# A two-model forward pass on one core: the first layer's index stage with its low products, key scalings, score relus and bias table copy in another order

## What is computed

```
proj = h @ w_in
q = rms_norm(proj[..., :o1].reshape(b, s, A_HEADS, A_HEAD_DIM), q_gain)
k = rms_norm(proj[..., o1:o2], k_gain)
v = proj[..., o2:o3]
qi = proj[..., o3:o4].reshape(b, s, IDX_HEADS, IDX_DIM)
ki = proj[..., o4:o5]
wi = proj[..., o5:]
...
dots = jnp.einsum('bqhd,bsd->bqhs', qib, ki).astype(jnp.float32) * (IDX_DIM ** -0.5)
score = jnp.einsum('bqh,bqhs->bqs', wib.astype(jnp.float32) * (IDX_HEADS ** -0.5),
                   jax.nn.relu(dots))
score = jnp.where(admiss[None], score, NEG)
_, idx = lax.top_k(score, n_top)
...
bias = rel_bias[t5_bucket(idx - t[None, :, None])]
logits = logits + jnp.transpose(bias, (0, 3, 1, 2)).astype(jnp.float32)
```

## Time and profile before

| what | value |
|---|---|
| median of 3 runs | 1145.93 us (1145.24 to 1149.59) |
| profiled execution, its own time | 1146.56 us |
| its span in the profile | 1144.8 us |
| mean granted TensorE clock | 0.993 |
| TensorE matmul busy | 1115.6 us, 97% |
| TensorE weight load busy | 988.1 us, 86% |
| VectorE busy | 709.9 us, 62% |
| ScalarE busy | 583.5 us, 51% |
| GpSimd busy | 147.3 us, 13% |
| moved by DMA | 193.96 MB, mean 169 GB/s |

### The profile page before, as it was taken

One profiled execution on the slowest core, in us unless ns is written; L12 is line 12 of the kernel. 1 busy time (PEld: TensorE's weight loads), 2 busy tenths in 40 slices (PEclk: granted clock), 3 DMA queues, 4 the chain that ended last, 5 costly groups with the idle time before them and its releaser, 6 DMA issues.

```text
span 1144.8 us, 17804 instructions
## 1 busy us (share of the span) xinstructions
PE 1115.6 (97%) x7045; PEld 988.1 (86%) x7045; DVE 709.9 (62%) x995; ACT 583.5 (51%) x767; POOL 147.3 (13%) x106
## 2 busy tenths in 40 slices
PE   8999999999998999999999999999999999999997
PEld 7768888888887888888888999898899989999996
DVE  5863665656677646555556978476587655554554
ACT  5574644444677554444455546445546346443443
POOL 3534200000364240000030000000000022000001
PEclk9999999999998999999999999999999999999999
DMA  7927465555341236555555655437554444655552
GB/s 232 302 67 182 162 218 188 185 201 187 117 145 67 84 113 223 199 191 193 183 162 169 221 153 166 129 118 239 178 165 138 159 151 156 211 181 188 188 175 90
DMA packets 138782, 193.96 MB, mean 169 GB/s; under 512 B 7147, under 2 KB 112840, under 8 KB 138716
## 3 DMA queue, kind: packets, MB, share of 16 engines
q1 hardware_dynamic: 126796, 181.92, 48.9%
q10 hardware_dynamic: 11312, 11.05, 3.6%
q0 software_dynamic: 608, 0.08, 0.1%
HBM read 191.90 MB, written 6.37 MB: 173 GB/s over the span
## 4 chain that ended last, share of the span: by engine, by line
PE 81%; DVE 7%; ACT 6%; issue 2%; DMA 2%; POOL 1%; SPq 0%; ACTq 0%; DVEq 0%
PE psum L546 20%; PE psum L547 19%; PE psum L548 19%; PE psum L707 11%; PE psum L708 5%; ACT arena L1553 3%; PE psum L635 2%; ACT whi L1567 2%; DVE wlo L2123 2%; DMA raw<-in_a_w_in 2%; POOL wlo L1536 1%; PE psum L1265 1%; PE psum L1238 1%; PE psum L666 1%; DVE psum L2492 1%
## 5 line engine op out<-in xcount | busy, mean ns | idle before, releaser
L1567 ACT ACTIVATE whi<-raw 128x2048 fp32r<-128x2048 f32 (+2 forms) x174 | 325.8, 1874 | 259.7 <-PE psum L548 163.8
L2123 DVE TENSOR_TENSOR wlo<-raw,whi 128x2048 fp32r<-128x2048 f32 (+1 forms) x148 | 337.8, 2284 | 190.0 <-ACT whi L1567 189.0
L546 PE MATMUL psum<-xA,whi 128*128 128x256 f32 x840 | 240.5, 286 | 4.3 <-POOL wlo L1536 2.0
L547 PE MATMUL psum<-xA,whi 128*128 128x256 f32 x840 | 238.3, 284 | 0.0
L548 PE MATMUL psum<-xA,wlo 128*128 128x256 f32 x840 | 238.2, 284 | 0.0
L1536 POOL TENSOR_TENSOR wlo<-raw,whi 128x288 fp32r<-128x288 f32 (+3 forms) x57 | 117.2, 2082 | 805.2 <-ACT whi L1567 805.0
L707 PE MATMUL psum<-xA,whi 128*128 128x512 f32 x512 | 182.9, 400 | 0.1
L546 PEld LDWEIGHTS psum<-xA,whi 128*128 128x128 f32 x840 | 161.0, 192 | 7.9 <-DVE wlo L2123 3.8
L547 PEld LDWEIGHTS psum<-xA,whi 128*128 128x128 f32 x840 | 161.2, 192 | 0.7
L548 PEld LDWEIGHTS psum<-xA,wlo 128*128 128x128 f32 x840 | 161.1, 192 | 0.1
L546 PE MATMUL psum<-whi,xC 128*128 128x512 f32 (+1 forms) x384 | 149.7, 390 | 1.1 <-DVE xC L2432 1.1
(11 more groups left out here) (272 smaller groups left out, 1343.8 us busy)
## 6 DMA issues: line engine op xcount, KB each, us to landing
raw<-in_w_in SPq DMA_DIRECT2D x42, 1024.0 KB, 5.2
raw<-in_mlp_w_up SPq DMA_DIRECT2D x32, 1024.0 KB, 5.4
raw<-in_mlp_w_down SPq DMA_DIRECT2D x32, 1024.0 KB, 4.9
raw<-in_w_gate SPq DMA_DIRECT2D x11, 1024.0 KB, 5.3
raw<-in_w_up SPq DMA_DIRECT2D x11, 1024.0 KB, 5.3
raw<-in_w_down SPq DMA_DIRECT2D x11, 1024.0 KB, 4.9
raw<-in_a_w_in SPq DMA_DIRECT2D x6, 1024.0 KB, 7.1
raw<-in_a_w_o SPq DMA_DIRECT2D x4, 1024.0 KB, 4.9
```

The source lines that it names most:

```text
L546: nc.tensor.matmul(out, lh, rh, start=start, stop=False, skip_group_check=skip)
L547: nc.tensor.matmul(out, lh, rl, start=False, stop=False, skip_group_check=skip)
L1567: nc.scalar.activation(whi[c % N_SPLIT][:, 0:n], raw[c % N_RAW][:, 0:n], ACT.Copy).then_inc(hi_sem, 1)
L2123: V.tensor_tensor(wlo[c % N_SPLIT][:, 0:n], raw[c % N_RAW][:, 0:n], f(whi[c % N_SPLIT][:, 0:n]), ALU.subtract).then_inc(lo_sem["dve"], 1)
```

## The change

On TensorE, `qi0` is written out: all its high products (L866 of the new program, 32) come first and wait only for the high part of the weights; its 16 low products (L871) follow. The scores of heads 4 to 7 are computed behind the first query block of `q0a` and no longer before it, and the banks of `queries` are opened one by one. On ScalarE, the root of the key mean stands ahead of the splits of `qi1` and `q0a`; the relus of heads 0 and 1 stand ahead of the split of `q0b`; the skew copy is issued behind the relus of heads 2 and 3; the reading back into `toep` is issued behind the split of `q1b` and no longer before it. On VectorE, the low part of `qi1` comes behind the key scalings and the key mean.

```diff
@@ -856,7 +856,22 @@
-            feature_major("qi0", xA, 5)
+            c = index["qi0"]
+            hi, lo = slot(c, KT, 256)
+            pe.wait_ge(hi_sem, c + 1)
+            out = open_bank("qi0.0", 5)
+            for nt in range(2):
+                for k in range(KT):
+                    for part in range(2):
+                        nc.tensor.matmul(out[:, nt * 256:nt * 256 + 256], hi[:, k, nt * P:nt * P + P], xA[:, part, k, :],
+                                         start=nt == k == part == 0, stop=False, skip_group_check=True)
+            weights(c)
+            for nt in range(2):
+                for k in range(KT):
+                    ins = nc.tensor.matmul(out[:, nt * 256:nt * 256 + 256], lo[:, k, nt * P:nt * P + P], xA[:, 0, k, :],
+                                           start=False, stop=k == KT - 1, skip_group_check=True)
+            close_bank(ins, "qi0.0")
+            chunk_done[c] = full["qi0.0"]
@@ -885,17 +900,23 @@
             feature_major("qi1", xA, 1, between=first_dots)
-            wait_read("qi1.0")
-            dots((4, 5, 6, 7), (4, 5, 0, 2))
-
-            def queries(j, banks, before_last=None):
-
-                outs = [open_bank(f"q{j}.{blk}", b) for blk, b in enumerate(banks)]
+
+            def last_dots():
+                wait_read("qi1.0")
+                dots((4, 5, 6, 7), (4, 5, 0, 2))
+
+            def queries(j, banks, before_last=None, behind_first=None):
+
+                outs = []
                 for part in range(2):
                     c = index[f"q{j}{'ab'[part]}"]
                     hi, lo = slot(c, 4, 512)
                     weights(c)
                     for blk in range(NB):
+                        if not part:
+                            if blk and behind_first:
+                                behind_first()
+                            outs.append(open_bank(f"q{j}.{blk}", banks[blk]))
@@ -917,7 +938,7 @@
-            queries(0, (3, 6))
+            queries(0, (3, 6), None, last_dots)
@@ -1694,11 +1715,9 @@
             run(sd, ms, ACT.Sqrt, done["A.sd"])
-            split_to("q0a")
-            act.wait_ge(s_tab, 16)
-            shift_rows(tab_a, skew_a, 16)
             act.wait_ge(*done["A.k.ms"])
             run(hd[:, 0:2], hd[:, 0:2], ACT.Sqrt, done["A.k.sd"])
+            split_to("q0a")
@@ -1713,16 +1732,20 @@
             run(vecs[:, :], psum[:, bank["vecs"], 0:V_ROWS], ACT.Copy, read["vecs"])
+            index_relu(0)
+            index_relu(1)
             split_to("q0b")
-            for h in range(4):
-                index_relu(h)
+            index_relu(2)
+            index_relu(3)
+            act.wait_ge(s_tab, 16)
+            shift_rows(tab_a, skew_a, 16)
             evac_a("qi1.0", A["qiT"][:, 2:4, :])
             for h in range(4, IDX_HEADS):
                 index_relu(h)
             split_to("q1a")
+            split_to("q1b")
             act.wait_ge(s_skew, 16)
             act.dma_start(A["toep"], skew_a.ap().rearrange("h p s -> p h s")).then_inc(s_toep_a, 16)
-            split_to("q1b")
@@ -2251,7 +2274,6 @@
             run(V.reciprocal(rs, sd), done["A.rs"])
-            low_of("qi1")
@@ -2268,6 +2290,7 @@
             run(V.tensor_scalar(hd[:, 0:2], hs[:, 0:2], 1.0 / A_DIM, EPS, ALU.mult, ALU.add), done["A.k.ms"])
+            low_of("qi1")
             low_of("q0a")
```

## The result

| | before | after |
|---|---|---|
| median | 1149.29 us (21 runs, 1145.24 to 1157.32) | 1154.1 us (21 runs, 1152.0 to 1157.9) |
| ratio of after to before, 95% interval | | 1.0041 [1.0028, 1.0054] |
| profiled execution: own time, span | 1146.56, 1144.8 us | 1154.19, 1152.4 us |
| mean granted TensorE clock | 0.993 | 0.987 |
| table product to first attention scores | 15.56 to 60.10: 44.54 us | 16.84 to 67.84: 51.00 us |

The change makes the kernel 4.8 us slower by the medians. With more runs the kernel before came out at 1149.3 and no longer at 1145.9. The prediction said +0.3 and gave 1150.2 as the upper end of its range. The median of 1154.1 is outside that range; even the measured ratio, applied to the old 1145.9, gives 1150.6.

What follows compares the result with a forecast made beforehand. It took TensorE's path to the first attention scores, with four waits totalling 4.3 us, as the bound; 1.6 us won were given back on later VectorE and ScalarE chains, net +0.3: median 1146.3 us, 8 in 10 within 1144.2 to 1150.2.

Steps and rivals of the forecast that it cites:

- Edit 1: TensorE, `qi0`: with low products last, the 0.59 us wait goes; gain there 0.6 to 0.8 us.
- Edit 2: Key scalings ahead of `qi1`'s low part: a 2.9 us wait replaces 0.59 and 0.85; `qi1` starts 1.2 us later.
- Edits 3 and 4: Loads and ScalarE's order: `q0b` lands at 31.2, 1.6 us later; skew copy issued at 34.3, 11 us later.
- Edits 5 and 6: TensorE: waits of 1.7 us before the second scores and 1.12 us before `q1a` go; VectorE's choice starts 2.0 us later.
- one visible win: TensorE at `q1a`: starts at 46.45, 1.6 us ahead of 48.09.
- Edit 7: `q1b`'s load, issued at 38.05 beside the skew copy, takes 8.0 us; TensorE waits 0.8 us for its low part.
- Rival 3: `q1b`'s load takes 12.2 us, landing at 50.3; scaled queries at 60.5, +4.1 us, time 1150.4; chance 0.13.
- Edit 8: Skew copy takes 13.9 us, landing at 48.9; ScalarE waits 0.9 us, with masks and query normalisation queued behind.
- The sum: Whole kernel: +0.3 us, the 1.6 us won being given back before the turned queries; 1146.3 us for a median.
- the shift at 60: First attention scores at 60.4 against 60.10; everything behind moves with them as one block to the end.
- neither is shut out: DMA engines alternate between queues packet by packet, so skew copy and `q1b`'s load both get a share.

Runs made afterwards that it cites:

- e12: The changed kernel, unedited, profiled a second time; 1153.62 us, ratio 1.0042 to the kernel before.
- e8: The kernel before, with the eleven constant loads issued behind `q1b`'s load instead of `q0b`'s; 1147.77 us, ratio 0.9995.
- e5: The changed kernel with the skew copy behind the split of `q1b` and its reading back behind the second half of the queries; 1165.65 us, ratio 1.0142.
- e11: The kernel before, unedited, profiled a second time; 1146.26 us, ratio to itself 0.9983.
- e4: The kernel before with only the low products of `qi0` moved behind its high ones; 1149.63 us, ratio 1.0014.
- e6: The changed kernel with the skew copy back behind the split of `q0a` and `qi1` split ahead of the key-mean wait; 1151.17 us, ratio 1.0006.
- e10: The changed kernel: copy behind `q0a`'s split, `qi1` split early, constant loads behind `q1b`'s, 12 unread products ahead of `q1a`; 1152.06 us, ratio 1.0023.
- e3: The changed kernel with unread products on TensorE, 10 ahead of `qi1` and 18 ahead of `q1b`; 1149.35 us, ratio 1.0011.

## Why the prediction was wrong

- **Edit 1** was right: no wait, 32 high products straight on. Its 0.6 us won nothing, since edit 2's wait swallows them.
- **Edit 2** was right as to the wait (2.9 us said, 2.46 measured) and wrong as to its price. The prediction counted a wait as its length and said that `qi1` starts 1.2 us later, and left it there. The lower clock behind it added 1.5 us to the first half of `qi1`. In the frame of before the first scores stand at 30.04 instead of the 28.95 foreseen, and all that hangs on TensorE there is late by about as much: second scores at 37.37 (36.3), VectorE's choice at 42.6 (41.25), the load of `q1b` at 38.7 (38.05), `q1a` at 47.3 (46.45).
- **Edits 3 and 4**: no wait for `q0b`'s load, relus and copy in the order foreseen, 0.6 us later by the same clock. **Edits 5 and 6** were right: neither the second scores nor `q1a` wait. The "one visible win" of edit 6 was 0.8 us in the end (47.3 against 48.09).
- **Edit 7 is the step that failed.** "I take 8.0, `q1b`'s own ..., which is nearest: one load, the same copy." It measured 12.0, and 12.0 again in e12. The row was misread, and it was not one load: in before `q1a`'s load, issued ahead of `q1b`'s on the same queue, was in flight until 41.35, 5.2 of the 8.0 us, and by then the copy was all but through (2039 of its 2048 packets). In the new program no other load is in flight, but `q1b`'s is issued 3.8 us behind the copy instead of 12.9, in the copy's first part, where a load moves nothing for about 5 us. `q1a`'s 12.6 (5.5 us behind) was the nearer row. The prediction set it aside for its constant loads; e8 shows that they made nothing of it (12.9 without them). e5 shows the 5.2 us without the copy. TensorE's wait there was 4.24 us instead of 0.8.
- **Rival 3, "`q1b` lands late",** was therefore the case that came, with a chance of 0.13. Its chain is right to a few tenths: scaled queries foreseen at 60.5, measured at 62.06 less 1.28 = 60.8, and the mean of the query sums again ended with GpSimd's low part (58.54 and 58.50). But it gave +4.1 us, and the stretch lost 6.46. The rest is the clock behind the wait: 12 products in 5.29 us instead of 2.7, and a turning of 1.08 instead of 0.8, so that TensorE, and not the scaled queries, was the last to be ready.
- **Edit 8** was harmless: the copy landed within 15.8 us (13.9 was taken; its last packet moves 14.7 us after the issue), and ScalarE did not wait for it. In part that is luck: `q1b`'s load held ScalarE until 52.00, 50.7 in the frame of before, which is later than the 48.9 foreseen for the copy. The masks and queries were late because of `q1b`'s split ahead of them, and VectorE's and ScalarE's chains to the scaled queries ended ahead of TensorE.
- **The sum** then missed two terms: 3.4 us on the wait for `q1b`, and 3.99 us of lower clock, for which it had none. On the other side the wait before `qi1` was 0.4 shorter, and the 1.15 foreseen before the turned queries did not come. 0.3 + 3.4 + 4.0 - 0.4 - 1.15 = 6.15 of the 6.46; the terms overlap in part, so this is a reckoning and no proof.
- That the shift at 60 is carried whole to the end was right: 1084.7 against 1084.6 us behind it. That the two agree to 0.1 us is luck, as the same part takes 1085.7 in e11, 1083.9 in e12 and 1080.9 to 1086.0 in all.
- The 1145.93 of three runs was a low draw. In 21 runs the same kernel has 1149.29, and e11 shows two ways to such a spread: the lower clock ahead of the stage (1.7 us), and in it the order of the copy and `q0b`'s load (2.1 us), which is decided by less than a microsecond in each execution. How often it falls which way was not counted; only two executions have a profile.

The Trainium skill (DMA: Bandwidth & Descriptors, "Queues, rings and completion order") has each DMA engine go round between its queues packet by packet. The trace of after agrees for the second part of `q1b`'s load (268 packets of it beside 250 of the copy from 46 to 49 us), though the packets that the trace counts need not be those that the skill means. It does not agree for the first 5.7 us, in which the copy moves 1181 packets and the load none; there the measurement decides, and the prediction's "neither is shut out" was wrong. Of the 6.8 us that the load takes beyond e5's 5.2, 4.7 go by before its first packet and most of the rest is the slower going beside the copy. Why the first packet comes so late no run here shows.

What stays open is when a shorter wait costs the clock. The thirteen waits of 2.40 us and more in the stage were all followed by the lower one, and so was the 1.45 us of e4; those of 1.43 (e6), 1.67 (before), 1.97 (e8) and 2.06 us (e5) were not. Ahead of the stage, before the first weight products, seven profiles have a wait of 1.85 us, and five of them the lower clock behind it; the other seven wait 1.90 to 2.09 us and have none. So the length of the wait alone does not say it. Reading `toep` straight from `tab_a`, without the copy, was not tried.

## What to carry to other kernels

When a load's time is taken from a row, take a row in which it stands at the same distance behind the big transfer that is in flight and has the same loads in flight ahead of it on its own queue, and not the row with the same name; and before moving a big transfer, list the loads that will be issued in the ten microseconds behind it and which of them has slack. Price a TensorE wait of the size seen here (2.4 us and more) at its length and 1.2 to 2.8 us more for the lower clock behind it, unless other work can fill it. Where two engines issue transfers within a microsecond of each other, the order can differ from one execution to the next: profile the unedited kernel twice before reading an edit from one trace. And where a load is long, look at the packets of each queue: they tell a load that moves slowly from one that has not begun.

## What the runs showed of the hardware

- One 2 MB copy from DRAM to DRAM stretches the next 1 MB load from 5.2 to between 11.4 and 13.1 us if that is issued 1 to 5.5 us behind it, and hardly (5.4 to 6.2 us) if it is issued up to 1 us ahead or level. Issued 1.0 to 4.3 us behind, the load moves its first packet only 4.6 to 5.7 us after its issue (1.0 us without the copy), and from then on about as many packets as the copy (544 and 542 in 5 us of e10).
- The clock fell to 0.50 in or behind waits of 2.46 and 4.24 us and stayed there for 3.4 and 6.8 us. In another execution (e12) the same two waits (2.46 and 4.17 us) cost 2.6 us of busy time and not 4.0. With 10 and 18 products that nobody reads in the place of the waits (e3, the 18 in 4.24 us and 0.75 us of idle time behind them) it stayed at 1.00.
